# A gated delta rule in a two-layer trunk: the chunk inverse by substitution on GpSimd instead of the lower levels of block doubling, and the next step prepared inside the current one

## Reference

```python
def chunk_gated_delta(q, k, v, g, beta, s0):
    gc = jnp.cumsum(g_chunk, axis=-1)
    decay = jnp.where(tri, jnp.exp(gc[..., :, None] - gc[..., None, :]), 0.0)
    a_mat = jnp.where(strict, (k * beta) @ k.T * decay, 0.0)
    sol = triangular_solve(a_mat + I, [v * beta, k * beta * exp(gc)],
                           lower=True, unit_diagonal=True)
    a_qk = q @ k.T * decay
    # scan over the chunks
    u = u_base - w_dec @ s
    o = q_dec @ s + a_qk @ u
    s = s * c_dec + k_dec.T @ u
```

## Time and profile before

| | us |
|---|---|
| median of 3 runs | 2229.77 (2229.31 to 2233.7) |
| profiled execution | 2219.47 |
| its span | 2217.3 |
| PE busy | 1915.4 |
| DVE busy | 896.2 |
| ACT busy | 481.3 |
| POOL busy | 373.1 |

### The profile page before, as it was taken

One profiled execution on the slowest core, in us unless ns is written; L12 is line 12 of the kernel. 1 busy time (PEld: TensorE's weight loads), 2 busy tenths in 40 slices (PEclk: granted clock), 3 DMA queues, 4 the chain that ended last, 5 costly groups with the idle time before them and its releaser, 6 DMA issues. The chain is left out here.

```text
span 2217.3 us, 24642 instructions
## 1 busy us (share of the span) xinstructions
PE 1915.4 (86%) x9669; PEld 1300.0 (59%) x9669; DVE 896.2 (40%) x1686; ACT 481.3 (22%) x810; POOL 373.1 (17%) x280
## 2 busy tenths in 40 slices
PE   3899978978888895899679999888888889599975
PEld 2455655558888754444345566556888865444433
DVE  2179014565555424011237920546555541311114
ACT  1211013351111213122131101344111120322212
POOL 0001150043433102100111000005444300300001
PEclk8999897999999997899789999899999999699996
DMA  9322896800000003999562112530000000499953
GB/s 358 41 75 82 278 290 209 298 1 1 1 1 1 10 2 129 354 364 365 218 161 76 38 57 77 197 126 1 1 1 1 1 12 0 168 383 358 372 226 121
DMA packets 113920, 302.54 MB, mean 136 GB/s; under 512 B 27904, under 2 KB 35746, under 8 KB 100642
## 3 DMA queue, kind: packets, MB, share of 16 engines
q1 hardware_dynamic: 65424, 218.73, 26.7%
q0 software_dynamic: 14080, 53.48, 7.3%
q10 hardware_dynamic: 34322, 28.99, 4.6%
HBM read 235.09 MB, written 67.05 MB: 136 GB/s over the span
## 5 line engine op out<-in xcount | busy, mean ns | idle before, releaser
L626 PE MATMUL ps<-hreg,ring 128*128 128x512 f32 x768 | 400.2, 603 | 7.7 <-ACT hreg L1141 7.7
L627 PEld LDWEIGHTS ps<-hreg,ring 128*128 128x128 f32 x768 | 147.8, 192 | 187.6 <-issue 187.6
L986 PE MATMUL ps<-ring,tok 128*128 128x512 f32 x544 | 237.9, 595 | 0.2 <-issue 0.2
L986 PEld LDWEIGHTS ps<-ring,tok 128*128 128x128 f32 x544 | 103.9, 191 | 130.9 <-issue 130.9
L627 PE MATMUL ps<-hreg,ring 128*128 128x128 f32 x768 | 149.0, 276 | 0.0
L1969 POOL TENSOR_TENSOR hreg<-hreg,cst 128x512 f32<-128x512 f32 x70 | 88.9, 1270 | 301.7 <-DVE hreg L1674 254.7
L1001 PE MATMUL ps<-ring,work 128*128 128x512 f32 x272 | 123.7, 598 | 0.0
L626 PEld LDWEIGHTS ps<-hreg,ring 128*128 128x128 f32 x768 | 118.8, 195 | 8.0 <-issue 8.0
L1881 DVE TENSOR_TENSOR work<-work,ps 128x256 f32<-128x256 f32 x34 | 14.2, 421 | 252.5 <-ACT work L1364 252.5
L1503 DVE SCALAR_TENSOR_TENSOR mixA<-cin_reg,small,mixA 128x655 f32<-128x655 f32 x120 | 107.0, 895 | 0.0
L1687 DVE TENSOR_TENSOR hreg<-hreg,ps 128x512 f32<-128x512 f32 x50 | 34.3, 687 | 164.9 <-PE ps L846 164.9
(11 more groups left out here) (358 smaller groups left out, 3306.5 us busy)
## 6 DMA issues: line engine op xcount, KB each, us to landing
ring<-in_w SPq DMA_DIRECT2D x102, 1024.0 KB, 8.2
ring<-in_w_mod SPq DMA_DIRECT2D x24, 2048.0 KB, 8.6
ring<-in_w_in SPq DMA_DIRECT2D x12, 2048.0 KB, 9.0
ys<-zs ACTq DMA_DIRECT2D x34, 512.0 KB, 7.8
tok<-xs SPq DMA_DIRECT2D x30, 512.0 KB, 11.0
xs<-zero POOLq DMA_DIRECT2D x8, 1792.0 KB, 19.6
ys<-zero POOLq DMA_DIRECT2D x8, 1664.0 KB, 18.6
ring<-in_w_out SPq DMA_DIRECT2D x4, 2048.0 KB, 8.1
```

The costliest lines, as they stand in the source:

```text
L626: mm(o[:, 0:TS], lhs(k), rhs(k)[:, 0:TS], start=k == 0, stop=k == nk - 1)
L627: ins = mm(o[:, TS:T], lhs(k), rhs(k)[:, TS:T], start=k == 0, stop=k == nk - 1)
L986: ins = mm(bank(2 + q), xgT[q][:, k, :], w, start=k == 0, stop=k == KD - 1)
```

## The change

The matrix is first cut into its eight 16 x 16 diagonal blocks, and each of these is inverted by substitution, column by column, on GpSimd. That takes the place of levels 0 to 3. Levels 4 and 5 stay full doubling levels, level 6 works on the 64 x 64 halves alone (`last_w`, `last_x`), and `X` is no longer updated outside the half that level 6 needs.

- **Block substitution** (`diag_inverse`, GpSimd). Two masks of 128 x 512, two copies of 128 x 64, then 15 columns with a multiplication and a subtraction for each of the two directions, which alternate: 60 instructions of 4 x 15 down to 4 x 1 elements per partition, each of which waits for an earlier one of its own engine through `pool_step`.
- **Its input and its output.** `diag_rows` (PE, two parts of two 128 x 512 products with the block mask), four ACT copies (`diag_copies`), a DVE reduction and a DVE product of 128 x 1024 for each direction (`diag_spread`) lay the blocks out; `inverse_spread` (DVE), `turn_inverse` (PE) and `inverse_copies` (ACT) make `XT` and `X` from the result.
- **The masks of levels 4 and 5** are applied by DVE to the product in PSUM (`level_mask`), in place of GpSimd's masks and ScalarE's copies.
- **The next step is prepared inside the current one.** `CT`, `aqk`, `qdec` and `XT` have two buffers each. The products for step j + 1 stand between the levels of step j, on PE, DVE and ACT. Step 0 is prepared ahead of the loop.
- **Buffers.** PSUM banks 6 and 7 serve the preparation and banks 0 to 5 the levels and the recurrence. `XT` and the diagonal blocks lie in `ring[0]`. So SP loads the first expert's weights only after `dn_state` 10, the end of the fifth step.
- **Constants.** 14 level masks become 4, with three small tables added.

The core of the diff (`...` marks what is left out):

```diff
-LEV = 7
+BASE, LEVELS = 16, (4, 5)
...
-C_COL = C_LEV + 2 * LEV * P
+C_IND = C_LEV + 4 * P
+C_B8 = C_IND + P
+C_D16 = C_B8 + P // BASE
+C_COL = C_D16 + BASE
...
+        def half(reg, i):
+            return heads(reg[:, 512 * i:512 * i + 512])
+
+        B = [dict(DT=half(hreg, 5 * d), CT=[half(hreg, 5 * d + 1 + i) for i in range(2)],
+                  aqk=[half(hreg, 5 * d + 3 + i) for i in range(2)],
+                  qdec=[half(work, 3 * d + i) for i in range(2)], W=half(work, 3 * d + 2),
...
-                slot_free(("mod", mods_beside_attention(l)[-1]))
+                need(dn_state, 10)
...
+                def diag_rows(j, part):
+
+                    for d in range(2):
+                        if part == 0:
+                            need(dn_rhs, 2 * j + d + 1)
+                            need(dn_mat, 4 * j + 3 + d)
+                        else:
+                            need(dn_pcopy, 6 * j + d + 1)
+                        mm(pbank(d), cst[:, C_IND:C_IND + P], diag[d][:, 512 * part:512 * part + 512], start=True, stop=True)\
+                            .then_inc(dn_prep.sem, 1)
...
+                for j in range(5):
+                    level_w(j, 0)
                     if j < 4:
-                        decay_rows(j + 1)
-                    for d in range(2):
...
-                            mm(o, S[d][:, h, :], B[d]["qdec"][:, h, :], start=True, stop=False)
-                            mm(o, B[d]["W"][:, h, :], B[d]["aqk"][:, h, :], start=False, stop=True)
-                        for h in range(4):
-                            ins = mm(bank(4 * d + 1)[:, h * P:(h + 1) * P], B[d]["kdec"][:, h, :], B[d]["W"][:, h, :],
-                                     start=True, stop=True)
-                        ins.then_inc(dn_o.sem, 1)
+                        gram_kk(j + 1)
+                    level_x(j, 0)
+                    if j < 4:
+                        gram_kq(j + 1)
+                    level_w(j, 1)
+                    if j < 4:
+                        diag_rows(j + 1, 0)
+                    level_x(j, 1)
+                    if j < 4:
+                        diag_rows(j + 1, 1)
...
+                def diag_copies(j):
+                    for part in range(2):
+                        for d in range(2):
+                            need(dn_prep, 12 * j + 6 + 2 * part + d + 1)
+                            A_(diag[d][:, 512 * part:512 * part + 512], bank(6 + d), ACT.Copy).then_inc(dn_pcopy.sem, 1)
...
+                def diag_spread(j):
+
+                    for d in range(2):
+                        need(dn_diag, 2 * j + d + 1)
+                        got = count(V.tensor_reduce(dcomp[d], diag[d][:, 512:1024].rearrange("p (h b m) -> p h m b", h=4, m=BASE),
+                                                    AX, ALU.add))
+                    need(dve_step, got)
+                    rows_ = cst[:, C_D16:C_D16 + BASE].rearrange("p (a k b) -> p a k b", a=1, b=1).to_broadcast([P, 4, BASE, BASE])
+                    for d in range(2):
+                        V.tensor_tensor(diag4[d], dcomp[d].rearrange("p h (a m) -> p h a m", a=1).to_broadcast([P, 4, BASE, BASE]),
+                                        rows_, ALU.mult).then_inc(dn_rhs.sem, 1)
+
+                def inverse_spread(j):
+                    in_block = cst[:, C_B8:C_B8 + 8].rearrange("p (a k b) -> p a k b", a=1, b=1).to_broadcast([P, 4, 8, BASE])
+                    for d in range(2):
+                        need(dn_inv, 2 * j + d + 1)
+                        V.tensor_tensor(B[d]["XT"][j % 2].rearrange("p h (b m) -> p h b m", m=BASE),
+                                        dinv[d].rearrange("p h (a m) -> p h a m", a=1).to_broadcast([P, 4, 8, BASE]),
+                                        in_block, ALU.mult).then_inc(dn_xt.sem, 1)
...
+                for j in range(5):
+                    level_mask(j, 0)
+                    if j < 4:
+                        lower_mats(j + 1)
+                    level_add(j, 0)
+                    if j < 4:
+                        query_mats(j + 1)
+                        diag_spread(j + 1)
+                    level_mask(j, 1)
+                    level_add(j, 1)
...
                         need(dn_erow, 2 * j + d + 1)
-                        G.tensor_tensor(B[d]["qdec"], B[d]["qdec"], dnT[:, 0:4, a:a + P], ALU.mult).then_inc(dn_qk.sem, 1)
+                        G.tensor_tensor(B[d]["qdec"][j % 2], B[d]["qdec"][j % 2], dnT[:, 0:4, a:a + P], ALU.mult).then_inc(dn_qk.sem, 1)
+
+                def key_decay(j):
+                    for d in range(2):
+                        cc = chunk(j, d)
+                        if j:
+                            need(dn_seq, 6 * j - 1 + d)
                         G.tensor_tensor(B[d]["kdec"], heads(tok[:, 0, cc, :]),
                                         along(ekd[:, 20 * d + 4 * cc:20 * d + 4 * cc + 4], P), ALU.mult).then_inc(dn_qk.sem, 1)
...
+                def diag_inverse(j):
+
+                    for d in range(2):
+                        need(dn_mat, 4 * j + d + 1)
+                        G.tensor_tensor(heads(diag[d][:, 512:1024]), B[d]["CT"][j % 2], over_heads(cst[:, C_IND:C_IND + P]), ALU.mult)\
+                            .then_inc(dn_diag.sem, 1)
+                    at_ = [0, 0]
+                    for d in range(2):
+                        need(dn_pcopy, 6 * j + 3 + d)
+                        one_rows = cst[:, C_D16:C_D16 + BASE].rearrange("p (a m) -> p a m", a=1)
+                        at_[d] = counted(G.tensor_copy(dinv[d], one_rows.to_broadcast([P, 4, BASE])))
+                    for n in range(BASE - 1):
+                        left = BASE - 1 - n
+                        k_ = (n, BASE - 1 - n)
+                        to = (slice(n + 1, BASE), slice(0, left))
                         for d in range(2):
-
-                            if n == 2:
-                                need(dn_x, 2 * LEV * j + d + 1)
+                            need(pool_step, at_[d])
+                            k = k_[d]
+                            at_[d] = counted(G.tensor_tensor(dprod[d][:, :, 0:left], diag4[d][:, :, k, to[d]],
+                                                             dinv[d][:, :, k:k + 1].to_broadcast([P, 4, left]), ALU.mult))
+                        for d in range(2):
+                            need(pool_step, at_[d])
+                            ins = G.tensor_tensor(dinv[d][:, :, to[d]], dinv[d][:, :, to[d]], dprod[d][:, :, 0:left], ALU.subtract)
+                            if n < BASE - 2:
+                                at_[d] = counted(ins)
                             else:
-                                need(dn_w, 2 * (LEV - 1) * j + 2 * (n - 3) + d + 1)
-                            block_of(n, d)
+                                ins.then_inc(dn_inv.sem, 1)
+
+                query_decay(0)
+                key_decay(0)
+                diag_inverse(0)
+                query_decay(1)
+                for j in range(4):
+                    diag_inverse(j + 1)
+                    key_decay(j + 1)
+                    if j < 3:
+                        query_decay(j + 2)
+                assert steps[0] == POOL_STEPS, steps
+
```

340 lines of the change are left out of this document (207 added, 133 removed).

## The result

The changed kernel takes 2157.99 us (median of 4 runs, 2141.85 to 2168.05), the kernel before 2229.54 in the same comparison. The ratio is 0.9684, with a 95% interval of 0.9655 to 0.9712: 70 us faster, where the prediction said 90.5.

The account below looks back on a forecast made before the run. It took the delta-rule stage as the path, TensorE nearly bounding a level, GpSimd the new step: 217 + 15 + 8 = 240 us a layer, 89 saved in all, plus 1.5 at the start: 2139 us, range 2098 to 2225.

Parts of the forecast that it names:

- The forecast for the stage: Delta rule of each layer, to the last output: 240 us, 240.5 to the norm, down from 284.9.
- the 8 us a layer added for a dearer substitution: GpSimd's substitution: 0.18 instead of 0.155 us per small instruction, 5 x 61 x 0.025 = 8 us more.
- the signs named for being right: Delta-rule stage: lengths of stage, middle step and substitution, GpSimd starts, `inverse_spread` waiting for GpSimd, no new ScalarE wait, experts' start unchanged.
- I add 15, not 10: Stage of each layer: 15 us added to the laid-out 217 for what the layout left out, more gaps on PE.
- The rival with TensorE at 1.2 GHz: Delta-rule stage: half of TensorE's groups at 1.2 GHz, about 10 us a step, 2208 us in all; chance 0.08.
- A granted clock under 0.85 in the stage: TensorE in the delta-rule stage: one of the signs that would show the prediction wrong.
- The layout: Instructions of each engine in new order, started when engine and semaphores allow: middle step 39.4 us, full stage 217 us.
- GpSimd sets the step from here on: Middle step: substitution 14.3 us beside a recurrence of 13.7, almost a tie, with GpSimd as the bound.
- The price of the small instruction: GpSimd's 60 small instructions a step: fixed 0.155 us plus 2.11 ns per element, taken as 0.18, 15.8 us altogether.
- The rule of the Trainium skill: GpSimd's substitution: about 102 cycles per small read, 0.68 us more per instruction, 41 us per step, kernel some 300 us slower.
- The opening and the last step: Ends of the stage: first state 70.6 us, its preparation having no cover; last step 28.3, with nothing to prepare.
- A bound that doesn't follow: Kernel time for small GpSimd instructions between 0.26 and 0.33 us: gain merely small, 2182 to 2225 us; chance 0.14.

Follow-up runs that it names:

- The first fillers: Changed kernel plus dummy TensorE products, three groups ahead of `diag_rows` part 0 and two ahead of `turn_inverse`: ratio 0.9501 to the kernel before, 2118 us.
- Half a substitution less: Every second substitution column left out of the kernel with fillers, VectorE's order and moved `key_decay`; output differs: ratio 0.9405, whole time not used.
- Half as much again: Changed kernel with each substitution product issued twice, 90 small GpSimd instructions a step instead of 60: ratio 0.9895 to the kernel before, 2206 us.
- the last experiment: Changed kernel with 700 unused columns (0.36 MB) given back to the constants table; PE's first parameter matmul came 1.4 us later, no kernel time given.
- all three changes: Changed kernel with the fillers, VectorE's new order and the moved `key_decay` together: ratio 0.9426 to the kernel before, 2102 us.
- VectorE's new order: Changed kernel with `diag_spread` ahead of `query_mats`, `query_mats` behind the solve, `gram_kq` behind `key_state`, no filler: ratio 0.9514 to the kernel before, 2121 us.
- the moved `key_decay`: Changed kernel with GpSimd's `key_decay` behind the next step's diagonal mask and `query_decay` ahead of the substitution: ratio 0.962 to the kernel before, 2145 us.

## Why the prediction was right, and where its sizes were off

The direction, the place and the range were right. The forecast for the stage, 240.5 us, was 17.7 too low. It is in part luck that the kernel's time came within 19 us: the 8 us a layer added for a dearer substitution weren't there, and they made up for a part of what the clock cost. Of the signs named for being right, four failed: the stage (230 to 250 us), the middle step (42 to 45), the starts on GpSimd (0.22 to 0.30 us apart, 0.155 to 0.26 measured), and that `inverse_spread` would wait for GpSimd in a middle step. The substitution, 13.5 to 14.0 us with its copies, is at the lower edge of 14 to 21.

The kernel before also waited: in each step 1.7 to 3.0 us ahead of its transpose (L829, released by GpSimd), not only the 0.5 to 1.1 us that the earlier trace rows show. PE in the last of its steps:

```profile
710.28 0.65 PE L829 MATMUL ps<-cst,hreg 128*128 128x128 f32 x4 [2.98 <-POOL hreg L1969]
713.29 2.07 PE L836 MATMUL ps<-hreg 128*128 128x128 f32 x8 [0.66 <-DVE hreg L1682]
718.17 1.06 PE L846 MATMUL ps<-hreg 128*128 128x128 f32 x8
```

From 713.29 to 718.17 three groups took 4.9 us instead of 2.7. By the same count the three middle steps of layer 0 lose 1.6 to 2.7 us each.

- **The clock and the ports, "I add 15, not 10", is the term that failed.** The first fillers take 24.9 us a layer off (258.2 to 233.3), by the clock alone. The collision of `inverse_spread` is 7.3 us over the kernel, some 4 a layer. Together 29, twice the term, in the profiled executions. The prediction argued from a ratio of gaps (9 us a step on PE) and from 10 us that its layout of the kernel before had missed. It didn't ask what stands behind each wait. The kernel before loses 1.6 to 2.7 us a step behind its waits, by the rows above. In the changed kernel two waits of a step, 2.8 and 3.4 us, have together 6 us of such loss behind them. The rival with TensorE at 1.2 GHz had the mechanism and gave 10 us a step; 6.2 were measured. It had 0.08, and half of it came true.
- **"A granted clock under 0.85 in the stage" was named as a sign of being wrong.** Over the stage it is 0.83, in both layers: the sign was met.
- **The layout was good.** Its middle step of 39.4 us holds no clock and no ports. With the clock at 1.00 the step takes 41.5, and about 1 of that is the collision. Its pieces against the changed kernel, by the rows above and one step's length of 47.65: end of the substitution to the end of level 4's first product 9.0 us (603.52 to 612.49) for 5.6, to level 5's second product 16.1 (its L883 starts at 580.98) for 14.9, to GpSimd's next copy 8.6 (L2152 at 589.55) for 4.6, copies and substitution 14.0 for 14.3. The third is level 5 and `diag_rows` at 1.2 GHz, almost wholly; in the first, 1.3 us are the decay rows at 1.2 GHz and 1.2 the collision.
- **"GpSimd sets the step from here on" was wrong by half a microsecond, and in what follows from it.** The tie was seen; the recurrence ends 0.5 us behind the substitution. Half a substitution less changes no middle step at a clock of 1.00. Half as much again makes VectorE wait 5.4 us in every middle step; three of the six got longer by 5 to 7 us, in the other three the clock gave most of it back.
- **The price of the small instruction was close and on the safe side.** It was to be 0.155 us and 2.11 ns per element, then 0.18. Measured from start to start: 0.26 us with 60 elements ((498.32 - 497.29) / 4), 0.155 with 4 ((509.36 - 509.05) / 2). That is a fixed part of 0.15 and 1.8 ns per element. So the 8 us of the raised price weren't there: 13.5 us with the copies, 15.8 forecast.
- **Short rows cost nothing of their own.** Four rows of one element take 0.155 us in all. The rule of the Trainium skill (GPSIMD Engine Reference, Performance pitfalls for Q7 kernels), by which each small read costs about 102 cycles, isn't borne out by these rows for this kind of instruction: by the prediction's estimate it would have added 0.68 us to each, and the longest start to start is 0.26.
- **The opening and the last step.** The first step's last output copy ends 83.5 us after the stage's start (473.05 to 556.50), and 77.2 us after it with the fillers; 70.6 were laid out. The last step takes 31.2 us from state update to state update (695.08 to 726.32), 28.3 were laid out.
- **The start.** 1.5 us forecast, 2.4 measured; the last experiment agrees with the table as its cause but doesn't show it. The stage starts 4.0 us earlier. In the kernels of the experiments, with the same code up to there, it starts anywhere from 470.0 to 477.1 us, so these 4.0 us aren't shown to be the change's.
- **The weights of the first expert** cost nothing, as forecast: their load is issued at 730.75 and the experts' first matmul starts at 865.0, 133.8 us behind the stage's end. Before it was 132.0.
- **Not forecast: 6.6 us between the stages.** Almost all lies in the last part: 327.7 us at a granted clock of 0.92 (1169.3 to 1497.0), where the kernel before has 321.0 at 0.95, with 1337 matmul records in both. No experiment changed anything there, and in those with the same routing the distance between the stages is 758 to 769 us; with all three changes it is 759.1, as before. So one execution against one can't tell 6.6 us there. The 20 us between the gain by the profiles and the gain by the medians go with the granted clock of the execution (0.884 in the one profiled, up to 0.897 in the others); what sets that clock stays open.
- **A bound that doesn't follow.** By the prediction's own formula a small instruction of 0.26 us gives a kernel of some 2187 us, not 2182. Nothing hung on it, since the price came out lower.

## What to carry to other kernels

In these kernels the waits of TensorE on the path (2.4 to 7.9 us in the middle steps) mostly cost twice: their own length, and work behind them at 1.2 GHz. In a forecast, list every single wait and what stands behind it, not only how much idle time there is in all. Then order the other engine's work so that what TensorE waits for comes first, or fill the wait with products into a free bank that end before it does. Where two engines tie in a step, more work on either one costs at once, while less work on one alone gives nothing. The clock can blur both: compare steps at the same granted clock, and look at all of them, in both layers, before taking one for the rule.

## What the hardware showed that was not expected

- One and the same step, with the same instructions in the same execution, took 47.5 us at a granted clock of 0.82 and 41.9 at 0.96, with the same waits of 2.41 and 3.41 us in it. Shifts of 1 to 3 us in another engine's order moved the changed kernel's 0.86 to 0.92 and above in most steps.
- After 1.96 us of idling `diag_rows` part 0 still took 2.26 us, as at full clock in the kernel with VectorE's new order; after 3.41 us it took 2.97. In the last middle step of the kernel with half as much substitution again it took 2.26 after 3.42 us, too. After 4.49 us, in the kernel with the moved `key_decay`, it took 3.61, but level 5 behind it was at full clock there. So the length of the wait alone doesn't decide it.
- Forty dummy instructions more on TensorE made a step 6.2 us shorter.
- 60 dependent GpSimd instructions on 128 x 4 to 128 x 60 elements took 12.3 us, 0.2 us each, in pairs on separate data with waits on the engine's own semaphore.
- A 128 x 512 product of VectorE from SBUF took 0.68 us alone; a pair of them beside two of GpSimd took 1.05 and 1.53 us.
